# Second layer's attention in a chained two-block kernel: modulation weights and high halves move to ScalarE, the softmax maximum is negated by its own reduction

## The reference

```python
def memory_attention(q, mem_kv):                     # both layers of the first block, 4 heads of width 64
    k, v = mem_kv[..., :X_WIDTH], mem_kv[..., X_WIDTH:]
    s = jnp.einsum('bshd,bmhd->bhsm', q, k) * (X_HEAD_DIM ** -0.5)
    p = jax.nn.softmax(s, axis=-1)
    return jnp.einsum('bhsm,bmhd->bshd', p, v)
...
proj = h @ w_in_b[j]                                 # second layer: q, k, v (768 wide each), memory query (256)
cross = memory_attention(mem_q, mem_n @ w_mem_kv[i])
...
ada = jax.nn.silu(c) @ ada_w[l] + ada_b[l]           # second block: 6 * 1024 columns
sh1, sc1, g1, sh2, sc2, g2 = jnp.split(ada, 6, axis=-1)
```

## Time and profile before

| what | value |
|---|---|
| median of 3 runs | 3530.3 us (3527.74 to 3534.25) |
| the profiled execution: its time | 3533.98 us |
| the profiled execution: its span | 3532.2 us |
| granted TensorE clock over the span | 0.970 |
| first layer's projections | 62 to 255 us |
| second layer's attention projections | 870 to 1016 us |
| stick-breaking attention behind them | 1016 to 1115 us |

### The profile page before, as it was taken

One profiled execution on the slowest core, in us unless ns is written; L12 is line 12 of the kernel. 1 busy time (PEld: TensorE's weight loads), 2 busy tenths in 40 slices (PEclk: granted clock), 3 DMA queues, 4 the chain that ended last, 5 costly groups with the idle time before them and its releaser, 6 DMA issues.

```text
span 3532.2 us, 34520 instructions
## 1 busy us (share of the span) xinstructions
PE 3192.2 (90%) x12438; PEld 2144.7 (61%) x12438; DVE 2228.2 (63%) x4218; ACT 758.0 (21%) x1510; POOL 1947.3 (55%) x1202
## 2 busy tenths in 40 slices
PE   7999999999999999999999999899988877787776
PEld 6778878887766788868877667444433323333332
DVE  4756552335865433369646776786778787777775
ACT  3462341112145311120131432011001110001000
POOL 3453349996602699968867555344444444444442
PEclk9998999999999999999999999999999999999999
DMA  4340022222320222323413123999999999999997
GB/s 159 138 160 1 1 72 96 95 95 90 125 95 25 84 96 100 113 72 117 143 66 120 37 88 123 412 404 421 408 401 422 422 421 421 421 419 413 411 422 317
DMA packets 108526, 745.75 MB, mean 211 GB/s; under 512 B 11992, under 2 KB 11992, under 8 KB 19544
## 3 DMA queue, kind: packets, MB, share of 16 engines
q0 software_dynamic: 73728, 536.90, 36.8%
q1 hardware_dynamic: 31024, 200.34, 16.1%
q10 hardware_dynamic: 3624, 6.56, 0.5%
HBM read 735.37 MB, written 8.39 MB: 211 GB/s over the span
## 4 chain that ended last, share of the span: by engine, by line
PE 61%; DMA 20%; DVE 9%; POOL 4%; issue 3%; ACT 2%; DVEq 0%; POOLq 0%; ACTq 0%
DMA arena<-in_peer_uv,rstd 15%; PE bank L1240 12%; PE bank L1241 12%; PE bank L1242 12%; PE bank L1746 8%; DMA weight_ring<-in_peer_uv,rstd 3%; POOL split_arena L1018 1%; DMA normed<-in_peer_uv,rstd 1%; POOL split_arena L1020 1%; DVE arena L3129 1%; PE bank L1676 1%; PE bank L1658 1%; PE bank L1534 1%; PE bank L1424 1%; PE bank L1761 1%
## 5 line engine op out<-in xcount | busy, mean ns | idle before, releaser
L1103 POOL DMA_INDIRECT arena<-in_peer_uv,rstd x419 | 475.1, 1134 | 641.2 <-PE bank L1746 585.2
L1242 PE MATMUL bank<-split_arena 128*128 128x512 f32 x1776 | 698.5, 393 | 0.0
L3129 DVE CUSTOM_DVE_ANT_0 arena<-arena,branch 128x1024 f32<-128x1024 f32 x419 | 512.8, 1226 | 263.2 <-DMA arena<-in_peer_uv,rstd 260.6
L1018 POOL TENSOR_TENSOR split_arena<-weight_ring,ones 128x1024 fp32r<-128x1024 f32 x208 | 515.3, 2477 | 200.2 <-PE bank L1242 144.7
L1240 PE MATMUL bank<-split_arena 128*128 128x512 f32 x1392 | 551.2, 396 | 15.7 <-DVE split_arena L2480 9.8
L1241 PE MATMUL bank<-split_arena 128*128 128x512 f32 x1392 | 544.7, 391 | 0.0
L1020 POOL TENSOR_TENSOR split_arena<-weight_ring,split_arena 128x1024 fp32r<-128x1024 f32 x208 | 529.0, 2544 | 16.3
L1746 PE MATMUL bank<-arena,level_mask 128*128 128x512 f32 x840 | 410.7, 633 | 111.1 <-DVE level_mask L3110 111.0
L1746 PE MATMUL bank<-arena,row_diagonals 128*128 128x512 f32 x836 | 391.6, 610 | 70.5 <-DVE row_diagonals L3110 70.2
L1242 PEld LDWEIGHTS bank<-split_arena 128*128 128x128 f32 x1776 | 336.0, 189 | 74.6
L1746 PEld LDWEIGHTS bank<-arena,level_mask 128*128 128x128 f32 x840 | 162.5, 201 | 338.2 <-issue 170.3
(11 more groups left out here) (457 smaller groups left out, 4942.0 us busy)
## 6 DMA issues: line engine op xcount, KB each, us to landing
weight_ring<-in_w_up SPq DMA_DIRECT2D x32, 1024.0 KB, 4.8
weight_ring<-in_w_down SPq DMA_DIRECT2D x32, 1024.0 KB, 4.8
weight_ring<-in_w_in SPq DMA_DIRECT2D x32, 1024.0 KB, 4.9
weight_ring<-in_ada_w SPq DMA_DIRECT2D x24, 1024.0 KB, 4.9
weight_ring<-in_w_in_a SPq DMA_DIRECT2D x12, 1024.0 KB, 6.7
weight_ring<-in_w_out SPq DMA_DIRECT2D x12, 1024.0 KB, 6.7
weight_ring<-in_w_in_b SPq DMA_DIRECT2D x10, 1024.0 KB, 6.1
weight_ring<-in_peer_wq SPq DMA_DIRECT2D x10, 1024.0 KB, 9.3
```

The costliest lines, as they stand in the source:

```text
L1018: pool.tensor_tensor(hi, part, bc_mid(ones[:], DT), ALU.mult).then_inc(split_hi, 1)
L1103: pool.indirect_dma_start(row_slots[slot_of[r]], None, a["peer_uv"], bass.IndirectOffsetOnAxis(ap=experts[n % 2][:, c:c + 1], axis=0)).the ...
L1242: return pe.matmul(psum[t.bank][:], hi, a_lo[k], start=False, stop=last)
L3129: dve.tensor_tensor_reduce(row, row, h_tok[:, r // NE, :], 1.0, 0.0, ALU.mult, ALU.add, dots[:, i % 4, j:j + 1]).then_inc(dot_ready, 1)
```

## The change

For units B2 to B6 ACT writes the high halves and POOL only the low ones (B0 and B1 stay with POOL). Units A0 to A9 are scaled on ACT by 8 activations each of 128 x 256; DVE keeps the reduction. ACT takes A0 right behind the 8 activations L2122, A1 to A6 between the cross steps, and A7, A8 and A9 before it empties the first bank of a v product. In both layers the memory keys are scaled by 1/8 when they are copied out of PSUM, the exp takes scale 1, and the row maximum is written negated by the reduction, so that L2530 is gone.

```diff
+ATTN_OWN = 2
...
-        split_units(attn_units)
+        split_units(attn_units[0:ATTN_OWN])
+        split_units(attn_units[ATTN_OWN:], True)
...
-                        split_half(u, h, attn_w, waits, u.own + h + 1)
+                        if u.high is None:
+                            split_half(u, h, attn_w, waits, u.own + h + 1)
+                        else:
+                            low_half(u, h, attn_w)
...
-                                           bias=soft[:, 0, 2 * b + n:2 * b + n + 1], scale=XD ** -0.5,
+                                           bias=soft[:, 0, 2 * b + n:2 * b + n + 1], scale=1.0,
...
-                    take(key_tiles[l][h], memk[:, l, h, :], width=NMEM)
+                    t = key_tiles[l][h]
+                    full(act, t)
+                    act.activation(memk[:, l, h, :], psum[t.bank][:, 0:NMEM], ACT.Copy, scale=XD ** -0.5).then_inc(
+                        bank_out[t.bank], 1)
...
+            def attn_high(i):
+                if i < len(attn_halves):
+                    u, h = attn_halves[i]
+                    v, g = attn_halves[i - HALVES]
+                    act.wait_ge(half_done, 2 * v.u + g + 1)
+                    high_half(u, h, attn_w)
+
+            def scale_modulation(u):
+                act.wait_ge(landed[u.slot], 16 * u.load)
+                for k in range(DT):
+                    m = act.activation(raw(u)[:, k, :], raw(u)[:, k, :], ACT.Copy, scale=c_col[:, k:k + 1])
+                m.then_inc(mod_scaled, 1)
+
+            scale_modulation(layer_ada[0])
+            for i in range(2 * ATTN_OWN, HALVES + 1):
+                attn_high(i)
             full(act, factor_turn)
             act.activation(rstd_tok[:], psum[factor_turn.bank][:, 0:TT], ACT.Copy).then_inc(bank_out[factor_turn.bank], 1)
+            ada_at = 1
             for i in range(len(sq_tiles)):
+                attn_high(HALVES + 1 + i)
+                while layer_ada[ada_at].u < attn_all[1 + (i + 1) // 2].u + 2:
+                    scale_modulation(layer_ada[ada_at])
+                    ada_at += 1
                 for what, x in beside(i):
                     cross_step(1, what, x)
+            for u in layer_ada[ada_at:]:
+                scale_modulation(u)
             have(act, factor_turn)
             for i, t in enumerate(sv_tiles):
...
-                if u.layer:
-                    dve.wait_ge(landed[u.slot], 16 * u.load)
-                    dve.tensor_tensor(raw(u), raw(u), bc_last(c_col[:], UNIT_N), ALU.mult).then_inc(mod_scaled, 1)
                 dve.wait_ge(mod_scaled, u.ada + 1)
...
-                    ch.link(dve.tensor_reduce(soft[:, 2, 2 * b:2 * b + 2],
-                                              psum[t.bank][:].rearrange("p (n m) -> p n m", m=NMEM), AX_X, ALU.max))
-                    dve.tensor_scalar(soft[:, 0, 2 * b:2 * b + 2], soft[:, 2, 2 * b:2 * b + 2], -XD ** -0.5, None,
-                                      ALU.mult).then_inc(neg_max, 1)
+                    dve.tensor_reduce(soft[:, 0, 2 * b:2 * b + 2], psum[t.bank][:].rearrange("p (n m) -> p n m", m=NMEM), AX_X,
+                                      ALU.max, negate=True).then_inc(neg_max, 1)
```

More of the change, by code:

```diff
@@ L2124, in _ @@
             act.activation(lb[:], lb[:], ACT.Exp).then_inc(lb_exp, 1)
+            attn_halves = [(u, h) for u in attn_units for h in range(2)]
+            layer_ada = [u for u in ada_units if u.layer == 1]
+            def attn_high(i):
[12 more added lines that the diff above has]
+                attn_high(i)
             full(act, factor_turn)
             act.activation(rstd_tok[:], psum[factor_turn.bank][:, 0:TT], ACT.Copy).then_inc(bank_out[factor_turn.bank], 1)
+            ada_at = 1
             for i in range(len(sq_tiles)):
+                attn_high(HALVES + 1 + i)
+                while layer_ada[ada_at].u < attn_all[1 + (i + 1) // 2].u + 2:
+                    scale_modulation(layer_ada[ada_at])
+                    ada_at += 1
                 for what, x in beside(i):
                     cross_step(1, what, x)
+            for u in layer_ada[ada_at:]:
+                scale_modulation(u)
             have(act, factor_turn)
```

## The result

The change makes the kernel slower by 0.3%: median 3538.0 us (3532.1 to 3546.2, 20 runs) against 3526.5 us (3519.4 to 3537.8, 20 runs) for the kernel before on the same chip. The ratio is 1.0031 (95%: 1.0022 to 1.0040), so about 10.9 us. A second set of 12 runs gave 1.0028 (1.0015 to 1.0040). I had forecast +5.2 us. The direction and the place of the loss were right; of its size I had half. The outcome to which I gave 0.64, a change within 0.2%, did not come; "slower by over 0.2%" did, with 0.30. That the time itself lies 2.5 us from my 3535.5 is in part luck: the kernel before, which I took at 3530.3, has its median at 3526.5 here.

What follows compares the result with a forecast made beforehand. TensorE, busy 90% of the span, bounds the kernel; only its waits count. First layer -2.3, A0/A1 -1.5 and A9's wait +9.0 sum to +5.2 us: 3535.5 us from a median of 3530.3, range 3528 to 3543.

Steps and rivals of the forecast that it cites:

- One unit on ScalarE, 3.3 us: Scaling one A unit by eight ScalarE activations was to take 3.3 us, bounds 2.7 and 5.0.
- The rival of small activations at full pitch: At A0 and A9, a unit takes 5.0 instead of 3.3 us, giving 3538.9 us; chance 0.30.
- A0 4.0 us later, gap 5.8: Second layer's projections: A0's sum runs 4.0 us later, so PE's gap before it becomes 5.8 us instead of 1.8.
- A9 ahead of the v banks, 9.0 us: B9's v product: PE waits 6.8 us for a bank emptied only after A9, plus 2.2 clock loss: 9.0 lost.
- The rival that the wait doesn't reach PE: At A9 before the v product, the 9.0 us loss is gone: 3526.5 us; chance 0.12.
- High halves and A2 to A6, nothing: B2 to B6's high halves on ScalarE and A2 to A6's scaling: PE didn't wait there, so no gain or loss.
- First layer, 2.3 us: Dropping L2530 at head 0 wins 1.5 us, shorter waits at later heads 0.8: 2.3 us won, bounds 1.0 and 6.4.
- the rival of the whole release: First layer: L2538 doesn't wait for POOL and no low clock comes at 90: 4.1 us less, 3531.4; chance 0.12.
- Sum: before 9.5, after 5.8 + 2.2 = 8.0: 1.5 us won: Second layer at A0 and A1: PE's gaps and low clock fall from 9.5 to 8.0 us, A1's gap closing.
- Before's 9.5: PE's loss at A0 and A1 in the kernel before: gaps of 1.78 and 2.62 us plus 5.1 of low clock.
- After's 2.2: Clock loss taken behind the one long gap at A0 after the change: 2.2 us, none at A1.
- The rival "slower": Slower by over 0.2%: units at A0 and A9 take 5.0 us, longer low clock adds to it; chance 0.30.

Runs made afterwards that it cites:

- e7: The changed kernel with A0 alone scaled by VectorE as before: 3531.7 us, ratio 1.0009 against the kernel before.
- e5: The kernel before with only A7 to A9 scaled by ScalarE ahead of the v evacuations: 3537.6 us, ratio 1.0027.
- e6: The kernel before with only the high halves of B2 to B6 written by ScalarE: 3524.5 us, ratio 0.9992.
- e10: The kernel before with the softmax part, the first layer's two copies moved, and A0 scaled early by ScalarE and reduced ahead of the first projections: 3514.5 us, ratio 0.9964.
- e12: The kernel of e8 run again, nothing altered: 3514.7 us, ratio 0.9966 against the kernel before.
- e1: The kernel before once more, nothing changed: 3527.7 us, ratio 0.9997.
- e3: The kernel before with the softmax part alone (scaled keys, negated maximum, no L2530): 3523.3 us, ratio 0.9979.
- e8: The changed kernel with A0 scaled and reduced early, A7 to A9 scaled between v banks, first layer's two copies moved earlier: 3515.9 us, ratio 0.9961 against before.
- e11: The kernel before with the softmax part and the first layer's two copies moved, second layer's order unaltered: 3520.6 us, ratio 0.9980.
- e4: The changed kernel with A7 to A9 scaled between the v banks and A0 scaled by VectorE: 3522.9 us, ratio 0.9990 against before.
- e9: The changed kernel once more, nothing altered: 3537.6 us, ratio 1.0028 against the kernel before.

## Why the prediction was half right

- **One unit on ScalarE, 3.3 us.** Measured 3.28 to 3.31. The rival of small activations at full pitch (5.0) is out: eight take 0.40 each but for the last. The estimate by the Trainium skill's figures (ScalarE: Activation LUTs, section What ACT_TABLE_LOAD costs), 3.3, agrees.
- **A0 4.0 us later, gap 5.8.** Measured 5.77.
- **A9 ahead of the v banks, 9.0 us.** Measured 9.2 after, 9.1 in its repeat, 9.6 in e7 and 9.9 in e5, by a gap of 6.88 (6.8 forecast) and a clock loss that differs: 2.3 after (16.30 against 14.03 for the product, clock 0.50 from 999.2 to 1006.0), about 2.9 in e5 (0.50 from 990.7 to 1000.9, of which PE was busy for 5.86). The rival that the wait doesn't reach PE is out.
- **High halves and A2 to A6, nothing.** The times of e6, and of e10 against e12, agree, though "PE never waited for these halves" left out that VectorE waits for POOL at A1 (e6).
- **First layer, 2.3 us.** From the first split product to the last l2 sum 166.0 instead of 169.2, in the repeats 165.6 and 168.8: 3.2 us. L2569 took 3.31 us and ended 1.08 us behind POOL's instruction, at 80.39, as worked out, so the wait passed on to it, and the rival of the whole release is out in that point. The rule that I had cited from the Trainium skill (SBUF — State Buffer, section Who interferes with whom) agrees. The turn at 81.95 came at 80.63, 1.3 us earlier where 1.5 was forecast. The other point of that rival came true: no low clock at 90 to 95 (1.7 us), which I had kept as a bound only. The 0.8 us that I counted for later heads isn't there: VectorE's wait at 165.86 is gone, but a gap of 0.87 us opened at 171.04, ended by POOL (0.38 before). Nor is 169 a firm base: e5, with the old code there, took 166.9. The four traces with it average 168.4, the six with the softmax part in the old order 166.0: 2.4 us.
- **The step that failed: "Sum: before 9.5, after 5.8 + 2.2 = 8.0: 1.5 us won".** Two sizes in it were off. *Before's 9.5* was one execution's, and a long one. From A0's sum, A1's came 19.47 us later and the next sum 17.92 after that; in e1 17.28 and 16.31, in after 16.91 and 16.21. Against the trace that I had, the change does give 4.0 - 2.56 - 1.71 = -0.3 us; against e1, 4.0 - 0.37 - 0.10 = +3.5. *After's 2.2* for the clock was 3.4: 16.91 against the 13.51 of e12, which has neither gap nor low clock. With both mended the term is +3.5 instead of -1.5. e5 sides with e1 (17.19 and 16.31), so two traces of three have the shorter chain.

The sum by the measured terms is -3.2 + 3.5 + 9.2 = +9.5 us (+10.3 with 2.4 for the first layer); the timed difference is 10.9 (7.8 to 14.1) and, in the repeat, 0.28%, 9.9 us. So nothing else of size is needed.

The rival "slower" named the outcome, but not by its own way: its main price, a unit at 5.0 us, isn't there, and only its side remark on a clock that stays low longer is, at A0. The range held; its upper end, 3543, was wider than the terms named for it, which give 3535.5 + 2.9 + 3.4 = 3541.8.

And a thing that I hadn't split: the softmax part is the change's gain, 5 to 7 us (e3). By the traces some 2.4 lie in the first layer and 2.4 in A1's chain (34.0 against 36.4), where I had put the closing of the gap down to ScalarE's help. ScalarE's part is a loss of about 4 at A0 and 9 in the tail, and no time shows a gain against it. That loss is order, not work: with A0 early and the units between the banks (e8, e12) both gaps are gone.

Left open: whether the low clock at 246 us belongs to e11's order or to its one trace. And of the low clock I can tell where it follows a gap and what it costs, but not how long it will last: behind like gaps of 1.75 to 1.79 us it stayed low for 3.4 us (e3: 880.9 to 884.3; e5) or 6.8 (e4: 880.6 to 887.4; e1).

## What to carry to other kernels

Before moving work to an idle engine, write out that engine's order at the place and ask of each moved instruction what stands behind it: an instruction that waits for a load, ahead of the emptying of a bank, passes its wait on to whoever needs the bank (here 6.88 us of TensorE), however idle the engine is. Take the price of a stall that differs between executions from more than one of them, as from two traces and not the longest gap of one, and follow the chain from one fixed event to the next rather than the gap alone. And split a change of several parts in the forecast: a part that shortens the same chain (here the softmax) may already give what the costly part is meant to bring.

## What the hardware did that I had not expected

- A stretch of low clock came while TensorE was busy all the time. In the trace of before and in e9's, of 14, the clock is at its lower level for some 24 us. Before, then e9:

```profile
258.00:282.00 24.00, 24.00 (x77) 16.73 (x77) 17.24 (x38) 3.37 (x8) 6.89 (x5) 0.50 0.05 20
```

```profile
254.00:280.00 26.00, 25.87 (x91) 18.44 (x91) 18.00 (x39) 3.96 (x9) 8.43 (x6) 0.54 0.06 26
```

  PE issues 77 matmuls there in 24 us; in the trace of after it issues 135 from 258 to 282 us, at a clock of 0.93. From the last l2 sum to the turns L1187 x20, these two traces take 96.2 us each, e1 90.6 and after 90.7: it costs 5.5 us of one execution, half of what the change does, as the others have a short low stretch there too (3.4 us in e1 and after). The profiled execution of before was 7.5 us above the median of 3526.5; this is most of it. DMA doesn't tell them apart (0.05 here, 0.00 in after). No run here shows what brings it.
- A two-number instruction of VectorE (L2530) lasted 0.17 to 3.26 us in the trace of before. The one of 2.94 in the earlier trace rows ended with POOL's instruction (79.11 and 79.09), and the two of e6 with POOL idle took 0.17. By it, A1's sum came 17.2 to 19.5 us behind A0's in executions with the same code there.
